# Layer 0's attention: one unrolled pipeline of 72 tiles in place of four loops of two heads

## The reference

```python
s = jnp.einsum('bhqmd,bhkmd->mbhqk', q2, k2).astype(jnp.float32) * (DK_A ** -0.5)
s = s + t5_bias(qpos, kpos, table)[None, None]
mask = (kpos[None, :] // CHUNK) <= (qpos[:, None] // CHUNK)
s = jnp.where(mask, s, NEG)
p = jax.nn.softmax(s, axis=-1)
a = p[0] - lam * p[1]
return jnp.einsum('bhqk,bhkd->bhqd', a.astype(v.dtype), v)
...
o = rmsnorm(o, subln) * (1.0 - lam_init)
y = o.transpose(0, 2, 1, 3).reshape(B, T, H_A * DV_A) @ w_o
```

## Time and profile before

| | us |
|---|---|
| median of 3 runs | 3531.21 (3526.49 to 3532.98) |
| profiled execution | 3527.08 |
| its span, first to last instruction | 3524.9 |
| PE busy in the span | 3322.1 (94%) |
| DVE, ACT, POOL busy | 2095.8 (59%), 1101.7 (31%), 959.5 (27%) |
| mean granted TensorE clock | 0.944 of full speed |
| chain that ended last, by engine | PE 80%, DVE 10%, issue 6%, ACT 3%, DMA 1% |

### The profile page before, as it was taken

The page is one execution under the profiler, slowest core; times in us unless marked ns, Lnnn a source line. Parts: engine busy times, 40 slices in busy tenths (PEclk is TensorE's granted clock), DMA queues, the critical chain, the costliest instruction groups (busy, mean ns, idle before and its releaser), DMA issues.

```text
span 3524.9 us, 51504 instructions
## 1 busy us (share of the span) xinstructions
PE 3322.1 (94%) x19213; PEld 3121.9 (89%) x19213; DVE 2095.8 (59%) x3289; ACT 1101.7 (31%) x2339; POOL 959.5 (27%) x526
## 2 busy tenths in 40 slices
PE   7999999999989999999988799998999999999997
PEld 5878888888779999999988688887899999999997
DVE  6454444444666565565676767775366656665675
ACT  3331333313442212222142146664232122221242
POOL 1102111121112222222233367775222222222231
PEclk8888887898899999999999899999999999999998
DMA  3111101110011111111110321113111111111111
GB/s 113 36 33 46 39 21 38 32 51 26 19 31 49 42 46 45 42 42 45 46 50 25 87 67 58 47 53 116 37 42 49 43 43 46 45 42 48 50 44 57
DMA packets 233439, 166.38 MB, mean 47 GB/s; under 512 B 25540, under 2 KB 212628, under 8 KB 233108
## 3 DMA queue, kind: packets, MB, share of 16 engines
q1 hardware_dynamic: 190712, 133.77, 12.7%
q10 hardware_dynamic: 42524, 29.70, 2.8%
HBM read 134.74 MB, written 28.70 MB: 46 GB/s over the span
## 4 chain that ended last, share of the span: by engine, by line
PE 80%; DVE 10%; issue 6%; ACT 3%; DMA 1%; ACTq 0%; POOL 0%; DVEq 0%; POOLq 0%
PE ps L705 24%; PE ps L707 22%; PE ps L706 22%; PE ps L791 3%; PE ps L817 3%; PE ps L838 2%; PE ps L906 2%; DVE t L1702 1%; DVE t L1588 1%; DVE t L1575 1%; ACT t L1290 1%; DVE t L1765 1%; DVE t L1708 1%; DVE t L1549 1%; PE ps L886 1%
## 5 line engine op out<-in xcount | busy, mean ns | idle before, releaser
L705 PE MATMUL ps<-t,t 128*128 128x384 f32 (+3 forms) x5144 | 1759.8, 342 | 52.0 <-DVE t L1575 12.1
L707 PE MATMUL ps<-t,t 128*128 128x384 f32 (+3 forms) x5144 | 1714.4, 333 | 0.0
L706 PE MATMUL ps<-t,t 128*128 128x384 f32 (+3 forms) x5144 | 1713.2, 333 | 0.0
L705 PEld LDWEIGHTS ps<-t,t 128*128 128x128 f32 (+1 forms) x5144 | 986.0, 192 | 126.1 <-DVE t L1575 35.4
L707 PEld LDWEIGHTS ps<-t,t 128*128 128x128 f32 (+1 forms) x5144 | 989.2, 192 | 7.6
L706 PEld LDWEIGHTS ps<-t,t 128*128 128x128 f32 (+1 forms) x5144 | 991.4, 193 | 3.1
L585 POOL TENSOR_TENSOR t<-t,t 128x1024 fp32r<-128x1024 f32 x205 | 533.3, 2602 | 1266.7 <-ACT t L1359 1261.4
L579 POOL TENSOR_TENSOR t<-t,t 128x1024 fp32r<-128x1024 f32 x75 | 151.4, 2019 | 1049.4 <-PE ps L707 1031.4
L1549 DVE TENSOR_TENSOR t<-t,ps 128x384 f32<-128x384 f32 (+1 forms) x624 | 310.6, 525 | 186.3 <-PE ps L707 184.3
L1807 DVE TENSOR_SCALAR t<-t 128x2 f32 (+1 forms) x88 | 16.8, 191 | 437.2 <-ACT t L1385 437.2
L1359 ACT ACTIVATE t<-t 128x1024 fp32r<-128x1024 f32 x130 | 138.0, 1061 | 413.7 <-PE ps L707 413.7
(11 more groups left out here) (152 smaller groups left out, 3122.2 us busy)
## 6 DMA issues: line engine op xcount, KB each, us to landing
t<-in_w_ffn_in SPq DMA_DIRECT2D x88, 512.0 KB, 3.8
t<-in_w_ffn_out SPq DMA_DIRECT2D x44, 512.0 KB, 3.6
t<-in_w_qkv_a SPq DMA_DIRECT2D x24, 512.0 KB, 3.9
out<-t ACTq DMA_DIRECT2D x24, 512.0 KB, 3.3
t<-in_w_ple_gate SPq DMA_DIRECT2D x16, 512.0 KB, 3.8
t<-in_x_prompt ACTq DMA_DIRECT2D x8, 512.0 KB, 7.6
t<-in_w_o_a SPq DMA_DIRECT2D x8, 512.0 KB, 3.7
t<-in_w_q_b SPq DMA_DIRECT2D x8, 512.0 KB, 4.3
```

The source lines that it names most:

```text
L705: pe.matmul(out, a_hi, b_hi, start=start, stop=False, skip_group_check=True)
L706: pe.matmul(out, a_hi, b_lo, start=False, stop=False, skip_group_check=True)
L707: return pe.matmul(out, a_lo, b_hi, start=False, stop=stop, skip_group_check=True)
```

## The change

Stage A becomes one list of 72 tiles, n = 9h + t, on each engine, and one projection behind it. Per tile PE does, in this order: transposes of the probabilities of n-2; scores of n, both maps side by side (rows 0 to 63 into banks 0 and 1, rows 64 to 127 into banks 2 and 3), then the bias; the first half of one product job of the head being prepared (`AT_STEP`, bank 7); values of n-2; transposes of tokens or cached keys in some tiles (`TOKENS`); the turn of the output of n-3; the second half of the job. Transposes share banks 4 and 5 in turn. Jobs for segments 1 and 2 of the same head stand in tiles 0 to 5, and Q, K, V of segment 0 of the next head in tiles 6 to 8.

POOL splits the next head's weights in tiles 4 to 6, K's low parts (L1765 was DVE's), the bias and the outputs. QKV weights have one raw buffer (`qkv_raw`) and three split ones. The output of a head goes to DRAM in three pieces per head (seven heads) and comes back after the last product job into the memory that held the normalised input; then eight column jobs of w_o run on all heads, and DVE adds 24 times to x. The loads and stores that ACT issued are SP's now.

```diff
+TILES_A = 72
+AT_STEP = (("K", 1), ("Q", 1), ("V", 1), ("K", 2), ("Q", 2), ("V", 2), ("Q", 0), ("K", 0), ("V", 0))
+TOKENS = {0: ("V", 0), 1: ("K", 1), 3: ("V", 1), 4: ("K", 2), 5: ("C", 0), 6: ("V", 2), 8: ("K", 0)}
...
+    kind, s = AT_STEP[t]
+    head = h + (t >= 6)
+    return (kind, head, s) if head < HA else None
...
+            def qkv_chunk(kind, h):
+
+                j = 3 * h + kind
+                if j:
+                    sp.wait_ge(qkv_split, j)
+                n0 = 1024 * (1, 0, 2)[kind] + 128 * h
+                sp.dma_start(qkv_raw[:, :].rearrange("p (k n) -> p k n", n=P),
+                             w_qkv_a[0].rearrange("(k p) n -> p k n", p=P)[:, :, n0:n0 + P]).then_inc(qkv_loaded, 16)
...
+            sp.wait_ge(job_done, 72)
+            for s in range(3):
+                sp.wait_ge(oa_stored[s], 32 * 7)
+            for h in range(7):
+                load_output_a(h)
+            for c in range(2, 8):
...
+            def split_qkv(kind, h):
+
+                j = 3 * h + kind
+                pool.wait_ge(qkv_loaded, 16 * (j + 1))
+                if h:
+                    pool.wait_ge(job_done, job_number("KQV"[kind], h - 1, 2) + 1)
+                pool.tensor_tensor(qkv_hi[kind], qkv_raw, zero.broadcast_to([P, CHUNK]), ALU.add).then_inc(qkv_round, 1)
+                pool.wait_ge(qkv_round, j + 1)
+                pool.tensor_tensor(qkv_lo[kind], qkv_raw, qkv_hi[kind].bitcast(F32), ALU.subtract).then_inc(qkv_split, 1)
...
+            def split_output_a(h, s):
+
+                a, w = SEGS[s]
+                j = 3 * h + s
+                pool.wait_ge(ot_kept, 9 * h + 3 * s + 3)
...
+            for n in range(TILES_A + 4):
+                h, t = divmod(n, 9)
+                if t == 0 and h:
+                    split_output_a(h - 1, 1)
+                if t == 3 and h:
+                    split_output_a(h - 1, 2)
+                job = job_at(n)
+                if h < HA and job is not None and job[0] == "K":
+                    keys_rest(job[1], job[2])
+                if h < HA - 1 and 4 <= t <= 6:
+                    split_qkv(t - 4, h + 1)
+                if h < HA and t == 6:
+                    split_output_a(h, 0)
+                if h < HA - 1 and t == 8:
+                    split_bias(h + 1)
...
-            def scores_a(t, m, uc):
-
-                e = 2 * t + m
-                if e >= 2:
-                    pe.wait_ge(exp_done, uc["s"](e - 1))
...
+            def turn_a(kind, index, srcs):
+
+                i = SLOT_A[kind, index]
+                if i >= 2:
+                    bank_kept(i - 2)
+                else:
+                    pe.wait_ge(rel_copied, 8)
+                for b, src in enumerate(srcs):
+                    m = pe.transpose(ps[:, 4 + i % 2, 128 * b:128 * b + 128], src, ident[:, :])
+                m.then_inc(t_done, 1)
...
+                    for term, (q, k) in enumerate(((q_hi, kh), (q_hi, kl), (q_lo, kh))):
+                        for m in range(2):
+                            rows = slice(64 * m, 64 * m + 64)
+                            pe.matmul(psf[:, 1024 * m + c0:1024 * m + c1], q[rows, a:b], k[rows, kc:kc + c1 - c0],
+                                      start=term == 0, stop=False, skip_group_check=True)
+                first, o = max(0, width - (256 if t < 8 else 192)), 256 - width
+                for m in range(2):
+                    for c0, c1, _, _, _ in pieces:
+                        b0 = max(c0, first)
+                        if b0 < c1:
+                            for part in (bias_hi, bias_lo):
+                                last = pe.matmul(psf[:, 1024 * m + b0:1024 * m + c1], ident_r[:, :], part[:, b0 + o:c1 + o],
+                                                 start=False, stop=part is bias_lo, skip_group_check=True)
+                    last.then_inc(s_done, 1)
+
...
+            def qkv_job(job, first, end):
...
+                for k in range(first, end):
+                    mm = three(ps[:, 7, 0:w], hi[:, 128 * k:128 * k + 128], lo[:, 128 * k:128 * k + 128],
+                               h_hi[:, k, a:a + w], h_lo[:, k, a:a + w], k == 0, k == KT - 1)
+                if end == KT:
+                    mm.then_inc(job_done, 1)
...
+                for n in range(TILES_A + 3):
+                    u = n - 2
+                    job = job_at(n) if n < TILES_A else None
+                    if 0 <= u < TILES_A:
+                        probabilities_a(u)
+                    if n < TILES_A:
+                        scores_a(n)
+                    if job is not None:
+                        qkv_job(job, 0, 4)
+                    if 0 <= u < TILES_A:
+                        values_a(u)
+                    if token_at(n) is not None:
+                        tokens_a(*token_at(n))
+                    if n >= 3:
+                        output_a(n - 3)
+                    if job is not None:
+                        qkv_job(job, 4, KT)
+
+            def project_a():
+
+                pe.wait_ge(oa_loaded, 16 * 14)
+                for j in range(8):
+
+                    def sum_free(s, j=j):
+                        if j == 0:
+                            pe.wait_ge(exp_done, 144)
+                            pe.wait_ge(oa_split, 21 + s + 1)
+                        else:
+                            pe.wait_ge(add_done, 3 * j + s - 2)
+
+                    column_jobs(j, 0, 0, sum_free)
...
+            for n in range(TILES_A + 3):
+                if 2 <= n < TILES_A + 2:
+                    probabilities_kept(n - 2)
+                if n < TILES_A:
+                    exponentials_a(n, 0)
+                    exponentials_a(n, 1)
+                if 2 <= n < TILES_A + 2:
+                    output_scale(n - 2)
+                if n < TILES_A:
+                    if n % 9 == 5:
+                        cached_keys_high(n // 9)
+                    if job_at(n) is not None:
+                        job_kept(*job_at(n))
 
...
+            for n in range(TILES_A + 3):
+                if n >= 3:
+                    output_scaled(n - 3)
+                if n < TILES_A:
+                    maximum_a(n, 0)
+                    maximum_a(n, 1)
+                    difference(n)
+                if 2 <= n < TILES_A + 2:
+                    output_kept(n - 2)
+                if token_at(n) is not None:
+                    tokens_kept(*token_at(n))
+                if n >= 3:
+                    output_turned(n - 3)
+                job = job_at(n) if n < TILES_A else None
+                if job is not None and job[0] == "Q":
+                    queries_low_a(job[1], job[2])
...
+            def add_columns(c0, g0, n):
+
+                between = squares_between(n)
+                for j in range(24):
+                    a, w = SEGS[j % 3]
+                    wait_column_job(c0 + j // 3, g0 + 2 * (j // 3), 0, 0, 0, j % 3)
+                    dve.tensor_tensor(x[:, j // 3, a:a + w], x[:, j // 3, a:a + w], ps[:, j % 3, 0:w], ALU.add).then_inc(add_done, 1)
```

More of the change, by code:

```diff
@@ L348, in reg, with stored_a @@
             return i * per + const
[L350 to L358, removed]
+        TB, FB, HB, VB = len(TURNED_A) + T_KVF, T_KVF, 8 * NG["A"], 8 * NG["A"]
+        def stored_a(s, heads):
+            return (32 if s == 2 else 16) * heads
         def scored(n, m):
@@ new lines, in _ @@
+            for kind in range(3):
+                split_qkv(kind, 0)
+            split_bias(0)
+            keys_rest(0, 0)
+            for n in range(TILES_A + 4):
+                h, t = divmod(n, 9)
+                if t == 0 and h:
[11 more added lines that the diff above has]
+                    split_bias(h + 1)
@@ new lines, in tokens_a @@
+            def tokens_a(kind, index):
+                if kind == "C":
+                    pe.wait_ge(kc_loaded, 16 * (index + 1))
+                    turn_a(kind, index, [kc_raw[:, b, :] for b in range(4)])
+                    return
+                raw, rawed = (k_raw, k_rawed) if kind == "K" else (v_raw, v_rawed)
+                s = index % 3
+                pe.wait_ge(rawed, index + 1)
+                turn_a(kind, index, [raw[:, a0 - 384 * s:a0 - 384 * s + 128] for a0, _ in BLOCKS[3 * s:3 * s + 3]])
@@ L799, in scores_a @@
                 a, b = columns(t)
-                lo, hi = 64 * m, 64 * m + 64
-                s0 = 1024 * m
+                width = 128 * (t + 1) if t < 8 else PAST + TS
                 if t < 8:
-                    pieces = [(c, min(c + 512, 128 * (t + 1)), k_hi, k_lo, c) for c in range(0, 128 * (t + 1), 512)]
+                    pieces = [(c, min(c + 512, width), k_hi, k_lo, c) for c in range(0, width, 512)]
                 else:
@@ new lines, in values_a @@
+            def values_a(n):
+                h, t = divmod(n, 9)
+                if n:
+                    pe.wait_ge(o_done, n)
+                if t % 3 == 0:
+                    pe.wait_ge(v_kept, 3 * h + t // 3 + 1)
+                if t == 8:
```

(11 more changed lines are left out.)

646 lines of the change are left out of this document (320 added, 326 removed).

## The result

The changed kernel takes 3360.4 us (median of 4 runs, 3356.17 to 3362.7), the kernel before 3529.78 beside it (3526.49 to 3532.98): a ratio of 0.9519 with a 95% interval of 0.9502 to 0.9535. The forecast was 3370 with 3315 to 3440. The profiled execution took 3362.7 us against 3527.1, 164.4 less.

What follows compares the result with a forecast made beforehand. Stage A was taken as bound by TensorE, with idle time and a lower clock. Eight heads of 79.7 us plus start, tail, projection and smaller terms gave 817.6 against 979.0, so 3370 us, range 3315 to 3440.

Steps and rivals of the forecast that it cites:

- The bound: Stage A, 936 us: without 54 of idle PE and 131 of lower clock 751, a gain of at most 185.
- Scores: 84 score matmuls a head at 11.0 us, between 15.4 without overlap and 9.5 with pairs costing one; switches 1.7.
- rival 2: The two 64-row score halves overlap wholly: scores 9.5, a head 78.2, 3358 us; chance 0.25.
- Waits between engines: PE waits over a head's nine tiles, taken from mixer B: 3.0 us a head, bounds 0 and 3.4.
- The pause: PE waits from the chain to tile 6's transposes, 2.3 us a head, and POOL's splits blocking DVE, 2.5.
- Head: One head of stage A: PE work 71.9, waits 3.0, stalls 2.3 and 2.5, sum 79.7 us.
- Start: Tile 0 starts at 69.0 us, after ACT's table load at 66.2, four copies and one DVE operation.
- Tail and projection: Stage A's end: tail 15.0 us after 4.5 of PE work counted already, projection 94.7, lower clock 2.0, normalisation 8.8.
- Costs put at nothing: Fewer additions to x, outputs' way through DRAM, the one raw weight buffer, DVE and ACT load: no time added.
- 1 (no overlap): The score halves don't overlap: scores 15.4, a head 84.1, 3405 us; chance 0.18.
- 3 (POOL blocks DVE in every tile): POOL's small splits block DVE in all nine tiles: 16.2 instead of 4.8, a head 91.1, 3461 us; chance 0.11.
- 4 (lower clock): PE's clock stays at the lower level in the heads; at 40% of their PE work 3600 us, slower; chance 0.04.

Runs made afterwards that it cites:

- the run with both edits: Changed kernel with cached keys turned and split in tile 2 instead of 5, and POOL's Q split waiting for tile 5's difference: 3322.1 us.
- the run with Q first: Changed kernel with cached keys in tile 2, next head's weights in order Q, K, V, each POOL split waiting for its tile's difference: 3300.4 us.

## Why the prediction was right

The time came out 10 us under the forecast, and the term sizes were off on both sides. By its own steps:

- **The bound.** "Without both the stage would take 751" named idle time and clock. The stage took 765.5, near it, but not by its two terms. Idle time rose by 23. By the same sum as the prediction's, at the clock of 0.94, 765.5 x 0.12/2 = 46 of the 131 us of the clock are still there; "a mean clock near 1.00" did not come, with 0.96 in the heads. That makes 85 - 23 = 62 of the 170.5 us. The other 108 or so, an estimate like the 46, are less PE work at the same level, which the bound left out. The run with the bias between the maps shows most of them: 76 us, and some 22 more that hid in shorter waits (19 us in six heads). What holds the clock up, the run with a quarter of the products shows. Its 154 us (205 - 51) are what products in waits save in the changed kernel, and no part of this sum. The moved DMA issues and the single projection were not tried apart.
- **Scores.** 11.0 with 1.7 for switches, 12.7, were forecast. Where the clock is up, they take 9.2 (the run with both edits, from the starts of each tile's first score and first bias). The halves overlap wholly: rival 2 was right on this term, and its rule with it; its 9.5 + 1.7 is still 2.0 too dear. The Trainium skill ("TensorEngine Tiling (Array Packing)", Key Properties) says that different tiles can multiply in parallel; the trace agrees, 3 to 17 ns from one map's start to the other's, and the run with the bias between the maps shows that a 128-row matmul there ends it.
- **Waits between engines.** 3.0 a head were forecast from mixer B; outside of tile 5's end there are 0.7 (before tile 5, behind L1916).
- **The pause.** Forecast were 2.3 for the chain and 2.5 for POOL's collision, three splits at half of 1.8. Measured: one pause of 5.3, and 2 more in tile 6 for the clock. The mechanism and place were right, with the sizes wrong: without the collision 1.86 of the pause are left (the run with Q's split behind the difference), for the chain's 2.3. The collision falls on one tile, as two of POOL's instructions one behind the other (1.35 on the ratio, 2.17 on the difference); the other two splits cost 1.0 on tile 4's ratio and nothing. And I had no term for the clock behind a pause. The Trainium skill ("SBUF — State Buffer", Terms) says that the loser is blocked for the whole instruction. The rows agree: the ratio ends within 0.03 us of POOL's first instruction, and the difference, 1.02 alone, 0.8 after the second.
- **Head.** 79.7 forecast, 77.5 measured: less for scores (3.5), bias (0.7) and waits (2.3), more for the pause with its clock (2.5) and for PE's products, transposes and values together (54.5 in the run with Q first, for 52.7).
- **Start.** 69.0 forecast, 74.87 measured. The step "ACT's table load ends at 66.2" took normalisation as unchanged; it ends at 72.7. But POOL's splits of Q and V fell on DVE's additions of squares: seven took 16.03 us, where they had taken 9.68. It is the same collision, at a place where I hadn't looked for it.
- **Tail and projection.** From the end of tile 71's scores and bias (683.9) to the first product 19.6, forecast 19.5; from there to the next stage 105.0, forecast 94.7 + 2.0 + 8.8 = 105.5.
- **Costs put at nothing.** The loads of outputs begin at 669.82 and no engine waits for them. Q's split was not late in the changed kernel. It became late by 1.57 us when it had to wait for the difference.
- **The other rivals.** 1 (no overlap) fell with the scores; 3 (POOL blocks DVE in every tile) with the groups by form, one difference of nine (and two ratios); 4 (lower clock) holds in the heads for one tile of nine only, 2 us a head.
- **Sums.** Two of the range's ends are added up a little off: stalls from nothing to their upper bound move the time by 8 x 4.8 = 38 and 8 x 5.2 = 42 us, where 43 and 35 stand. Nothing hangs on it.

So the number was right partly by luck, because errors met: scores, bias and waits between engines 6 to 7 us a head too dear, the pause with its clock 2 to 3, PE's other matmuls 2 a head and the start 6 us once too cheap.

## What to carry to other kernels

Work that is spread through a pipeline is worth what it covers: count the waits that it fills, and test it by leaving it out. When an engine is freed of a wait, look at what else the late engine has behind the same instruction (a bank, a second split, another buffer) before believing the sum, as here one edit gave 14, one 11 and both 38. Where GpSimd and VectorE both read SBUF, place GpSimd's long instructions by a wait on the VectorE instruction that they would block, and give them a producer early enough for it.

## What was not expected

- Three 64-row products of one half followed by three of the other still ran in pairs (mostly 6 to 17 ns apart), in spite of their order; a 128-row matmul between them kept them apart.
- VectorE's ratio, one column in and out (128x1), was blocked by GpSimd just as the wide difference was: up to 1.57 us instead of 0.22.
- Earlier loads of 1 MB of weights pushed the start of x's squares back by 3.8 us and took back 3.8 of the 6.4 that they saved.
